# Final RMSNorm of a two-layer decoder kernel: one square on VectorE, two row tiles scaled by GpSimd and ScalarE, another order of stores

## The reference

```python
def rms_norm(x, g):
    x32 = x.astype(jnp.float32)
    y = x32 * lax.rsqrt(jnp.mean(x32 * x32, axis=-1, keepdims=True) + EPS)
    return (y * g.astype(jnp.float32)).astype(x.dtype)
...
        ple_gate = jax.nn.sigmoid(rms_norm(h, norm_ple[i]) @ w_ple_gate[i])
        h = h + ple_gate * (p[i] @ w_ple_proj[i])
    return rms_norm(h, norm_final)
```

## Time and profile before

| what | value |
|---|---|
| median of 3 runs | 1206.46 us (1205.49 to 1207.88) |
| profiled execution, its own time | 1207.06 us |
| its span, first to last instruction | 1205.0 us |
| busy: TensorE / VectorE / ScalarE / GpSimd | 1156.7 / 893.5 / 742.3 / 137.4 us |
| last matmul of the gate product begins | 1194.71 us |
| last multiply of the final norm begins | 1201.3 us |

### The profile page before, as it was taken

How to read it: one execution, slowest core, us unless ns; L and a number is a source line. 1 busy time by engine, 2 the same in 40 slices (tenths; PEclk the granted TensorE clock), 3 DMA queues, 4 the chain that set the end, 5 groups by cost and what they waited for, 6 DMA issues and landing times.

```text
span 1205.0 us, 16841 instructions
## 1 busy us (share of the span) xinstructions
PE 1156.7 (96%) x5770; PEld 927.9 (77%) x5770; DVE 893.5 (74%) x1164; ACT 742.3 (62%) x910; POOL 137.4 (11%) x100
## 2 busy tenths in 40 slices
PE   5999999998999999999999998998999999999996
PEld 4778887786788888888778875686788888888775
DVE  5642346826799999999876439826799999999875
ACT  5553220233788788788656429734778788788654
POOL 0000000001121122121100000001121222121100
PEclk9999999999999999999999998999999999999999
DMA  9473212142699999999682311232699999999631
GB/s 380 171 312 105 70 35 71 35 175 107 221 350 394 378 374 383 374 374 389 246 333 70 106 35 37 73 137 106 214 355 385 377 377 390 374 376 386 258 139 70
DMA packets 50085, 287.58 MB, mean 239 GB/s; under 512 B 9216, under 2 KB 9216, under 8 KB 20721
## 3 DMA queue, kind: packets, MB, share of 16 engines
q1 hardware_dynamic: 34256, 243.06, 53.1%
q0 software_dynamic: 15776, 43.82, 9.8%
HBM read 272.68 MB, written 30.41 MB: 252 GB/s over the span
## 4 chain that ended last, share of the span: by engine, by line
PE 84%; DVE 8%; ACT 3%; DMA 3%; issue 2%; SPq 0%; POOLq 0%; DVEq 0%; ACTq 0%
PE psum L467 78%; PE psum L769 2%; DVE arena L2264 2%; ACT whi L1130 1%; DMA arena<-vscr,cur 1%; DVE arena L2277 1%; PE psum L810 1%; DVE wlo L1647 1%; DMA raw<-w_dense_dram 1%; PE psum L534 1%; ACT ahi L1130 1%; PE psum L698 1%; DVE alo L1703 0%; DMA arena<-yscr 0%; PE psum L1062 0%
## 5 line engine op out<-in xcount | busy, mean ns | idle before, releaser
L1647 DVE TENSOR_TENSOR wlo<-raw,whi 128x2048 fp32r<-128x2048 f32 x213 | 485.8, 2289 | 103.0 <-ACT whi L1130 92.6
L467 PE MATMUL psum<-whi,ahi 128*128 128x512 f32 (+1 forms) x1184 | 470.5, 397 | 11.5 <-issue 3.8
L467 PE MATMUL psum<-whi,alo 128*128 128x512 f32 (+1 forms) x1184 | 459.9, 388 | 0.0
L467 PE MATMUL psum<-wlo,ahi 128*128 128x512 f32 (+1 forms) x1184 | 458.9, 388 | 0.0
L1130 ACT ACTIVATE whi<-raw 128x2048 fp32r<-128x2048 f32 (+1 forms) x215 | 409.6, 1907 | 78.5 <-PE psum L467 75.0
L467 PEld LDWEIGHTS psum<-whi,ahi 128*128 128x128 f32 x1184 | 223.1, 188 | 60.0 <-issue 9.4
L467 PEld LDWEIGHTS psum<-whi,alo 128*128 128x128 f32 x1184 | 223.0, 188 | 46.6
L467 PEld LDWEIGHTS psum<-wlo,ahi 128*128 128x128 f32 x1184 | 223.5, 189 | 40.9
L1130 ACT ACTIVATE arena<-psum 128x512 f32<-128x512 f32 (+1 forms) x141 | 81.2, 586 | 144.4 <-PE psum L467 115.1
L1130 ACT ACTIVATE ahi<-psum 128x512 fp32r<-128x512 f32 x146 | 81.8, 593 | 83.2 <-PE psum L769 35.7
L467 PE MATMUL psum<-arena 128*128 128x512 f32 (+9 forms) x802 | 126.5, 331 | 4.5 <-DVE arena L1990 4.4
(11 more groups left out here) (188 smaller groups left out, 864.6 us busy)
## 6 DMA issues: line engine op xcount, KB each, us to landing
raw<-w_moe_dram SPq DMA_DIRECT2D x192, 1024.0 KB, 9.3
raw<-w_dense_dram SPq DMA_DIRECT2D x35, 1024.0 KB, 7.9
yscr<-arena POOLq DMA_DIRECT2D x2, 4096.0 KB, 23.2
arena<-yscr POOLq DMA_DIRECT2D x8, 1024.0 KB, 7.1
vscr<-arena POOLq DMA_DIRECT2D x8, 512.0 KB, 2.9
arena<-w_proj_dram POOLq DMA_DIRECT2D x2, 1024.0 KB, 6.3
arena<-gains_dram POOLq DMA_DIRECT2D x3, 512.0 KB, 3.6
out_dram<-arena SPq DMA_DIRECT2D x3, 512.0 KB, 2.6
```

What stands on the lines that cost most here:

```text
L467: return nc.tensor.matmul(o, l, r, start=start, stop=stop, **kw)
L1647: tt(wlo[:, b % SPL, :], raw[:, b % RAW, :], halves(whi[:, b % SPL, :]), ALU.subtract).then_inc(lo_ready, 1)
```

## The change

The second square of tile 3 is computed by VectorE as a tensor_tensor_reduce into the scratch area `AR_LAST2`; it raises `m["sg"]`, and ScalarE's root of tile 3 waits for that. For tiles 1 and 2 GpSimd multiplies `h` by the gain vector as soon as the tile is ready, VectorE computes only the reciprocal of the root, and ScalarE scales GpSimd's product by it in place. The stores then run in the order tile 0, tile 1, the halves of tile 3, tile 2. All values are computed as before, with the two multiplications of tiles 1 and 2 in another order.

```diff
--- before.py
+++ after.py
@@ -102,6 +102,7 @@
 AR_POS = (1024, 1536, 7680, 8192, 8704, 9216, 9728, 5632)
 AR_OUTS = (AR_OUT, AR_JUNK)
 AR_FIN = 0
+AR_LAST2 = 4096
 AR_I16 = AR_OH + TB * P // 2
 AR_LASTW = AR_I16 + P // 2
 TILES = [(i, q) for i in range(2) for q in range(TB)]
@@ -237,6 +238,7 @@
         s_xg = sems("s_xg", 2)
         s_sc = sems("s_sc", 2)
         y_zero = sem("y_zero")
+        n_hg = sem("n_hg")
 
 
         fnames = ("pos",
@@ -301,6 +303,8 @@
                 6: (g_H, 0), 7: (g_ob, 0), 8: (s_add, 0), 10: (M[0]["gt"], 0),
                 11: (M[0]["gt"], 4), 12: (t_z, 0), 15: (s_add, 4),
                 17: (M[1]["gt"], 0)}
+
+        HI = 2 * TB * len(ORDER)
 
         def nhalf(tb, half):
 
@@ -451,12 +455,15 @@
                 sp.dma_start(out[tb * P:(tb + 1) * P, cols], xn(6 * TB + tb)[:, cols])\
                   .then_inc(w_full[slot], 16)
 
-            for tb in range(TB - 1):
-                sp.wait_ge(n_xn, nrows(6, tb))
-                rows_out(tb, slice(0, D), tb)
+            sp.wait_ge(n_xn, nrows(6, 0))
+            rows_out(0, slice(0, D), 0)
+            sp.wait_ge(n_hi, HI + 1)
+            rows_out(1, slice(0, D), 1)
             for half in range(2):
-                sp.wait_ge(n_xn, nrows(6, TB - 1) + half)
+                sp.wait_ge(n_xn, nrows(6, 0) + half + 1)
                 rows_out(TB - 1, slice(half * 512, half * 512 + 512), TB - 1 + half)
+            sp.wait_ge(n_hi, HI + 2)
+            rows_out(2, slice(0, D), 2)
             for slot in range(TB + 1):
                 sp.wait_ge(w_full[slot], 16 * ((NCHUNKS - slot + RAW - 1) // RAW) + 16)
 
@@ -1544,9 +1551,15 @@
                     if q == 1:
                         halves_sqrt(6, 0)
                 halves_sqrt(6, 1)
-                for tb in range(2, TB):
-                    half_square(6, tb, 1)
-                    halves_sqrt(6, tb)
+                half_square(6, 2, 1)
+                halves_sqrt(6, 2)
+                act.wait_ge(m["sg"], TB + 1)
+                halves_sqrt(6, 3)
+                for tb in (1, 2):
+                    act.wait_ge(n_hg, tb)
+                    act.wait_ge(n_rec, 4 + tb)
+                    o = xn(6 * TB + tb)
+                    copy(o, o, scale=st[:, 6 * TB + tb, 2:3]).then_inc(n_hi, 1)
 
             tail(1)
             moe(0)
@@ -2162,8 +2175,16 @@
                     last_rows(0, 1)
                     gate(6)
                     gate(7)
-                    last_rows(1, 1)
-                    last_rows(2, 1)
+                    q = 6 * TB + TB - 1
+                    dve.wait_ge(h_ready, 6 * TB)
+                    o = h[:, TB - 1, 512:]
+                    nc.vector.tensor_tensor_reduce(out=area(AR_LAST2, 512), in0=o, in1=o, scale=1.0,
+                                                   scalar=0.0, op0=ALU.mult, op1=ALU.add,
+                                                   accum_out=st[:, q, 0:1]).then_inc(m["sg"], 1)
+                    for tb in (1, 2):
+                        dve.wait_ge(n_root, 6 * TB + tb + 1)
+                        nc.vector.reciprocal(st[:, 6 * TB + tb, 2:3], st[:, 6 * TB + tb, 1:2])\
+                            .then_inc(n_rec, 1)
                     last_rows(3, 2)
                     return
                 mix_lo(0, 0)
@@ -2430,6 +2451,11 @@
                         .then_inc(s_rows[tb], 16)
                 if layer == 1:
                     gain(6)
+                    pool.wait_ge(s_gain, 16 * SCALED[6])
+                    for tb in (1, 2):
+                        pool.wait_ge(h_ready, 5 * TB + tb + 1)
+                        nc.gpsimd.tensor_tensor(xn(6 * TB + tb), h[:, tb, :], area(AR_GAIN, D),
+                                                ALU.mult).then_inc(n_hg, 1)
                 else:
                     pool.wait_ge(h_ready, 2 * TB)
                     pool.dma_start(ar[:, AR_AC:AR_AC + ACONST_N], aconsts).then_inc(s_consts, 16)
```

## The result

| | before | change |
|---|---|---|
| median of 12 runs each | 1207.47 us (1205.49 to 1208.44) | 1210.38 us (1208.86 to 1211.73) |
| profiled execution, its own time | 1207.06 us | 1211.1 us |
| its span | 1205.0 us | 1209.3 us |
| start of the last sigmoid (gate 7) | 1195.30 us | 1196.41 us |
| **tail**: span less that start | 9.70 us | 12.89 us |

The change makes the kernel slower: the ratio is 1.0027, with a 95% interval of 1.0019 to 1.0035. That is 3.3 us (2.3 to 4.2) on 1207.47; the two medians lie 2.91 us apart.

What follows compares the result with a forecast made beforehand. The end was taken to follow tile 1's scaling, which starts the final store burst. GpSimd's products delaying VectorE, then tile 3's square, root and the first copy, add 3.45 to 1206.46: 1209.9 us, range 1206.9 to 1211.5.

Steps and rivals of the forecast that it cites:

- the sum: Delays along VectorE, GpSimd and ScalarE in the tail, up to the end of tile 1's scaling: +3.45 us.
- The bound: Last three tiles' stores leave as one full-rate DMA burst; the end is its start + 4.12 + 0.94 us.
- One for one: The kernel's time follows the end of tile 1's scaling by the same amount; that end moves +3.45 us.
- The product's length: Each 128x1024 two-input multiply on GpSimd takes 2.2 us, between 1.79 and 2.63; it counts twice.
- The turn: GpSimd's second product gets in between the two steps of tile 3's gate and holds VectorE until 1199.82 us.
- rival 2: GpSimd gets in only when VectorE has no two-input work ready, behind the square: about +1.5 us, 1208.0; chance 0.07.
- The square: Tile 3's second square on VectorE, a 512-column multiply with reduction, takes 0.74 us.
- The copy: ScalarE's scaled copy of 1024 columns, for tiles 1 and 2, takes 1058 ns each.
- The hole of 2.2 us: Expected sign: some 2.2 us between the two steps of tile 3's gate on VectorE, if the forecast is right.
- rival 1: GpSimd and VectorE read SBUF side by side; first copy only +0.58 us, 1207.0, no change; chance 0.16.
- Rival 3: GpSimd's first product starts late, freshly loaded code costing about 6 us: near +2.4 us or more; chance 0.06.
- Rival 4: Faster, if the store burst started before 1199.94 us; no gain over 0.2% seen; chance of faster 0.04.

Runs made afterwards that it cites:

- e6: Kernel before the change, with tile 1's store issued only when tile 2 is scaled; tail 11.02 us against 9.70.
- e4: Changed kernel with GpSimd's second product (tile 2) held back until VectorE's square of tile 3 is done; tail 13.52 us, ratio 1.0027.
- e9: Kernel before the change plus one unused 128x512 memset late on GpSimd, after tile 1's multiply; 1209.03 us, ratio 1.0012, tail 11.77 us.
- e10: Changed kernel with each GpSimd product replaced by h times a constant, so one SBUF input; tail 11.44 us against 12.89.
- e1: Changed kernel without GpSimd's two products, ScalarE scaling h itself; 1207.61 us, ratio 1.0005 to the kernel before the change, tail 10.32 us.
- e3: Changed kernel with only tile 1's product on GpSimd; VectorE scales tile 2 behind tile 3, stored last; tail 10.83 us.
- e4b: The changed kernel with GpSimd's second product held behind tile 3's square, run again several times; 1210.98 us, ratio 1.0027, tail 13.54 us.

## Why the prediction was right

The forecast was slower, with 1209.9 us in a range of 1206.9 to 1211.5; measured are 1210.38 us, and +3.3 us by the ratio where the sum had +3.45. The interval of the ratio, 0.19 to 0.35%, lies at and over the 0.2% that was named as the border.

- **The bound.** The end is the burst's start + 4.12 + 0.94 us: this held in the change (1204.2 + 4.0 + 1.1 = 1209.3) and in e6, where the store alone was moved. That the single terms came out 0.12 us shorter and 0.14 us longer and cancel is luck. "One for one" holds only for a later burst: before, tile 2's bytes already came some 0.1 us after the end of tile 1's, so by these rows an earlier tile 1 alone would have gained nothing. The bound did not hold in e4, e9 and e10, for a reason that the prediction did not have (below).
- **The product's length**, taken as 2.2 us: 2.39 us. Its start behind the add, taken as 0.30 us from a DMA issue: 0.16 us (1192.31 + 0.69 = 1193.00, then 1193.16). VectorE resumes before the product's row ends: tile 0's multiply ends at 1196.63, and 1.28 us back is 1195.35, 0.20 us ahead of the product's end at 1195.55. These three make gate 6 late by 0.90 + 0.19 - 0.14 - 0.20 = 0.75 us, which is what the rows show (1196.55, against 1194.69 + 1.11).
- **The turn.** The second product got in exactly where the sum had it, between the two steps of tile 3's gate: it is released inside the first step, waits, and holds the add. The hold is 2.03 us and not 2.2, again as VectorE resumes 0.13 us ahead of the product's end (1200.63 against 1200.76). That this end lies 2.20 us behind the step's (1198.56), as in the sum, is luck: the product takes 2.39 us, but its row is only 0.33 us longer (2.72), so it went on at about 1198.37, 0.19 us before the step's row ends. The place, drawn from the gather that got in between two back-to-back subtractions, was the step on which rival 2 hung; rival 2 is out.
- **The square**, 0.74 us from two smaller widths: 0.69 us, 0.05 us less. **The copy**, 1.06 us from a copy of another type: 1.13 us, 0.07 us more.
- **The sum**: -0.15 (lateness) - 0.17 (hold) + 0.02 (rounding of the steps between) - 0.05 (square) + 0.01 (root) + 0.07 (copy) = -0.27 us, and 3.45 - 0.27 = 3.18 us. The first copy ends at 1203.41, 7.00 us behind the last sigmoid, where tile 1's multiply ended 3.82 us behind it: +3.18. The tail has 3.19.
- **What was to be seen.** The hole of 2.2 us between the two steps isn't there. The add's row starts in its place and is 2.72 us long. A reader who looks for idle time would have found none and taken rival 1 for proven.
- **The rivals.** Rival 1 (side by side) falls with e1 and e3, but its sum for the rest of the change, +0.58, is confirmed by e1's +0.62. Rival 3 (a first product that starts late) falls by the 0.16 us. Rival 4 gave no gain, and none was found.
- **What I missed** is GpSimd's closing drain. The prediction priced GpSimd's work by who waits for its output, and an end of the program that waits for GpSimd itself was not among the cases. It did not matter to the forecast since the drain ended 1.1 us ahead of the closing semaphores. It makes rival 2 wrong in size: a product behind the square, for which the prediction had +1.5, gives +3.8 in the tail (13.52 - 9.70), no better than the collision that it avoids; over the runs the two kernels have the same ratio, 1.0027. The prediction's judgment that late work on GpSimd is covered by the burst was right only by that 1.1 us.

What stays open is in e10: why the row of a one-input instruction is longer and keeps VectorE out for less.

## What to carry to other kernels

Work that is moved to GpSimd is not off VectorE's path if it reads SBUF while VectorE has instructions with two SBUF inputs: one 128x1024 product held a 0.69 us add for 2.03 us, and it shows as a long row, so compare the mean length of the same instruction in two traces and not only the idle time. Ask what the end follows (here the start of the last burst, so tile 1's scaling) before the engines' loads are balanced; moving work off the last tile bought nothing. And look at what comes next: before, tile 2's bytes were already some 0.1 us late for the burst. Where GpSimd's drain set the end, the program ended some 7.4 us after GpSimd's last instruction (e9: 1206.9 less 1199.52; e4b: 1209.0 less 1201.55), so late work on GpSimd is free only if it ends earlier than that.

## What the runs showed of the hardware

- GpSimd's closing DRAIN ends 7.20 to 7.24 us after its last instruction, for each kind tried: a DMA issue (7.21), a memset (7.20, 7.21), a product (7.23, 7.24) or a multiplication by a constant (7.24). VectorE's takes 1.45 us in the kernel before, for two multiplies of 0.7 us each, so it ends with them.
- A VectorE instruction that is kept out starts on time in the profile and is long: 2.63 for 1.28 us, 2.72 for 0.69 us, 3.14 for 1.42 us (two), 1.99 for 0.69 us.
- The products keep VectorE's instructions with two SBUF inputs out by reading: a memset in a product's place costs nothing (0.69 us for the add), a VectorE add with one input in PSUM passes (0.69 us), and a VectorE square of one tensor by itself counts as two inputs (1.99 us). A GpSimd instruction with one SBUF input held the same VectorE instructions by 0.04 and 0.72 us only.
- VectorE goes on 0.13 to 0.20 us before the product's row ends, and GpSimd some 0.19 us before that of the VectorE instruction that it waited for.
- On GpSimd a 128x1024 float32 instruction took 0.95 us writing only (memset), 2.34 to 2.39 us with two inputs, and 2.79 us with one input and a constant, beside a VectorE multiply. The Trainium skill (GPSIMD Engine Reference, 3.1) has 4497 ns for a tensor_tensor add of 2048 columns, so 2.25 us as an estimate for 1024; the measured 2.34 to 2.39 us is slightly above that.
